# A three-group encoder layer on one core: the sums of a Strassen-like output product move from VectorE to GpSimd, ahead of the weight's low part

## What is computed

```python
h = rmsnorm(x, ln_gain[l])
proj = h @ w_in[l]
...
o_a = swa_sink_attention(q_a, k_a, v_a, q_norm_a[l], k_norm_a[l], sinks[l], bias)
o_c = short_gated_conv(b_c, c_c, x_c, conv_w[l])
mem_h = rmsnorm(mem, mem_ln_gain[l])
o_m = memory_cross_attention(q_m, mem_h, w_mem_kv[l], q_norm_m[l], k_norm_m[l])
mixed = jnp.concatenate([jax.nn.silu(g_a) * o_a,
                         jax.nn.silu(g_c) * o_c,
                         jax.nn.silu(g_m) * o_m], axis=-1)
x = x + mixed @ w_out[l]
```

## Time and profile before

| what | value |
|---|---|
| median of 3 runs | 2727.67 us (2726.12 to 2732.18) |
| the profiled execution | 2726.99 us |
| its span, first to last instruction | 2725.1 us |
| granted TensorE clock, mean | 0.996 of full speed |
| PE busy | 2666.0 us |
| DVE busy | 1686.9 us |
| POOL busy | 1496.5 us |
| ACT busy | 1101.5 us |

### The profile page before, as it was taken

How to read it: one execution, slowest core, us unless ns; L and a number is a source line. 1 busy time by engine, 2 the same in 40 slices (tenths; PEclk the granted TensorE clock), 3 DMA queues, 4 the chain that set the end, 5 groups by cost and what they waited for, 6 DMA issues and landing times.

```text
span 2725.1 us, 33717 instructions
## 1 busy us (share of the span) xinstructions
PE 2666.0 (98%) x12475; PEld 2198.8 (81%) x12475; DVE 1686.9 (62%) x2504; ACT 1101.5 (40%) x2435; POOL 1496.5 (55%) x1042
## 2 busy tenths in 40 slices
PE   6999999999999999999999999999999999999999
PEld 4888877888887778888877888888788788888887
DVE  4345775664476666456675754457642787867667
ACT  6333434442344344333434442343343444444443
POOL 5555644546554445555544455555454775756766
PEclk9999999999999999999999999999999999999999
DMA  7344443534344344334433434344245454444534
GB/s 216 122 138 124 159 135 97 174 110 161 106 138 151 112 143 142 129 119 140 159 120 113 155 124 139 113 132 151 92 150 168 157 199 146 167 150 140 174 118 140
DMA packets 234408, 383.16 MB, mean 141 GB/s; under 512 B 16822, under 2 KB 76292, under 8 KB 231940
## 3 DMA queue, kind: packets, MB, share of 16 engines
q1 hardware_dynamic: 189748, 274.05, 32.3%
q10 hardware_dynamic: 44496, 106.96, 11.1%
HBM read 308.86 MB, written 46.92 MB: 131 GB/s over the span
## 4 chain that ended last, share of the span: by engine, by line
PE 75%; DVE 13%; issue 3%; ACT 3%; DMA 2%; SPq 2%; POOL 1%; ACTq 0%; DVEq 0%
PE acc L1491 18%; PE acc L1493 17%; PE acc L1492 17%; DVE early L1146 4%; PE acc L1558 3%; PE acc L1562 3%; PE acc L1560 3%; ACT probs L779 1%; DMA probs_t<-blocks_t 1%; SPq L443 1%; PE ps_s L1615 1%; PE ps_o L1641 1%; DVE blocks_t L1221 1%; DMA raw<-in_w_mem_kv 1%; DVE a_lo L1362 1%
## 5 line engine op out<-in xcount | busy, mean ns | idle before, releaser
L536 POOL TENSOR_TENSOR w_lo<-raw,w_hi 128x512 fp32r<-128x512 f32 x928 | 1311.3, 1424 | 1168.6 <-ACT w_hi L620 1166.2
L620 ACT ACTIVATE w_hi<-raw 128x512 fp32r<-128x512 f32 x928 | 571.0, 628 | 1112.8 <-PE acc L1493 795.9
L1491 PE MATMUL acc<-h_hi,w_hi 128*128 128x512 f32 x1792 | 707.3, 395 | 12.8 <-POOL w_lo L536 10.7
L1492 PE MATMUL acc<-h_lo,w_hi 128*128 128x512 f32 x1792 | 700.4, 391 | 0.0
L1493 PE MATMUL acc<-h_hi,w_lo 128*128 128x512 f32 x1792 | 700.2, 391 | 0.0
L1491 PEld LDWEIGHTS acc<-h_hi,w_hi 128*128 128x128 f32 x1792 | 337.8, 188 | 91.6 <-POOL w_lo L536 13.8
L1493 PEld LDWEIGHTS acc<-h_hi,w_lo 128*128 128x128 f32 x1792 | 337.9, 189 | 70.9
L1492 PEld LDWEIGHTS acc<-h_lo,w_hi 128*128 128x128 f32 x1792 | 337.8, 189 | 68.7
L1491 PE MATMUL acc<-w_hi,h_hi 128*128 128x512 f32 (+1 forms) x1024 | 379.7, 371 | 0.0
L1493 PE MATMUL acc<-w_hi,h_lo 128*128 128x512 f32 (+1 forms) x1024 | 372.1, 363 | 0.0
L1492 PE MATMUL acc<-w_lo,h_hi 128*128 128x512 f32 (+1 forms) x1024 | 371.4, 363 | 0.0
(11 more groups left out here) (232 smaller groups left out, 3575.3 us busy)
## 6 DMA issues: line engine op xcount, KB each, us to landing
raw<-in_w_in SPq DMA_DIRECT2D x336, 512.0 KB, 4.0
raw<-w_sums SPq DMA_DIRECT2D x64, 512.0 KB, 3.9
probs_t<-blocks_t SPq DMA_DIRECT2D x384, 64.0 KB, 2.1
raw<-in_w_out SPq DMA_DIRECT2D x48, 512.0 KB, 3.6
stage<-in_w_out ACTq DMA_DIRECT2D x16, 1024.0 KB, 5.3
w_sums<-stage ACTq DMA_DIRECT2D x16, 1024.0 KB, 4.2
stage<-in_x ACTq DMA_DIRECT2D x16, 1024.0 KB, 5.1
mixed_rows<-ungated ACTq DMA_DIRECT2D x12, 1024.0 KB, 4.3
```

The costliest lines, as they stand in the source:

```text
L536: nc.gpsimd.tensor_tensor(w_lo[:, at, :], raw[:, slot_mod, HALF * half:HALF * half + HALF], w_hi[:, at, :].bitcast(F32), ALU.subtract).the ...
L620: nc.scalar.activation(w_hi[:, 2 * (slot_mod % 2) + half, :], raw[:, slot_mod, HALF * half:HALF * half + HALF], ACT.Copy).then_inc(hi_read ...
L1491: nc.tensor.matmul(dst, st[0], mv[0], start=first, stop=False)
L1492: nc.tensor.matmul(dst, st[0], mv[1], start=False, stop=False)
```

## The change

`a_sum` is taken from VectorE and given to GpSimd. It is called there ahead of `low` for the same slot. Its waits, its operands, and the semaphore that it raises stay as they were.

```diff
@@ gpsimd
+            def a_sum(j, h):
+
+                r, i, s = j // PAIR_SLOTS, j % PAIR_SLOTS // PRODUCT_SLOTS, j % PRODUCT_SLOTS
+                name, k = PRODUCTS[i][0], 2 * s + h
+                top, low = mixed_of[r // 2 * 2], mixed_of[r // 2 * 2 + 1]
+                s2 = low[:, k, :]
...
+                pool.wait_ge(s2_step, 16 * (r // 2 + 1))
+                pool.wait_ge(a_lo_ready, 2 * (j - 1) + h + 1)
+                nc.gpsimd.tensor_tensor(s_sum[:, h, :], *ins).then_inc(s_made, 1)
+
             for j in range(OUT_SLOTS):
                 if j + 2 < OUT_SLOTS:
+                    for h in range(2):
+                        a_sum(j + 2, h)
                     low((j + 2) % 4, OUT_BASE + j + 2)
@@ vector
-            def a_sum(j, h):
...
-                dve.wait_ge(s2_step, 16 * (r // 2 + 1))
-                dve.wait_ge(a_lo_ready, 2 * (j - 1) + h + 1)
-                nc.vector.tensor_tensor(s_sum[:, h, :], *ins).then_inc(s_made, 1)
...
                 if j + 2 < OUT_SLOTS:
-                    for h in range(2):
-                        a_sum(j + 2, h)
                     for h in range(2):
                         a_low(j + 2, h)
```

More of the change, by code:

```diff
@@ L587, in add_resid @@
                                         ALU.add).then_inc(resid_added, 1)
+            def a_sum(j, h):
[3 more added lines that the diff above has]
+                s2 = low[:, k, :]
+                if name == "S3":
+                    ins = (low[:, HALF_K + k, :], s2, ALU.subtract)
+                elif name == "S1":
+                    ins = (top[:, k, :], s2, ALU.add)
+                elif name == "S4":
+                    ins = (top[:, HALF_K + k, :], s2, ALU.subtract)
+                else:
+                    return
+                pool.wait_ge(s2_step, 16 * (r // 2 + 1))
+                pool.wait_ge(a_lo_ready, 2 * (j - 1) + h + 1)
+                nc.gpsimd.tensor_tensor(s_sum[:, h, :], *ins).then_inc(s_made, 1)
             for j in range(OUT_SLOTS):
                 if j + 2 < OUT_SLOTS:
+                    for h in range(2):
+                        a_sum(j + 2, h)
                     low((j + 2) % 4, OUT_BASE + j + 2)
```

## The result

The changed kernel takes 2758.43 us (median of 4 runs, 2754.93 to 2762.18) against 2729.26 us before (4 runs, 2726.12 to 2732.18). The ratio is 1.0107, with a 95% interval of 1.0086 to 1.0129. The forecast was 2756, range 2743 to 2776. The profiled execution took 2755.37 us with a span of 2753.6, against 2726.99 and 2725.1.

The account below looks back on a forecast made before the run. TensorE, busy 98% of the span, was taken as the bound. Late GpSimd costs 8.3 us a pair, 33.2 in four, less 4.9: +28.3 on 2726.99 gives 2755.3; with 0.7 for the median, 2756, range 2743 to 2776.

Parts of the forecast that it names:

- Price of an operation and of a collision: GpSimd in sum slots: 1.25 us an operation, plus 0.45 us for each VectorE operation with two SBUF inputs falling on it.
- The rival of full exclusion: GpSimd operations met by `a_lo`: each meeting costs the whole `a_lo`, 0.68 us; 30 us more, 2786; chance 0.03.
- First run: Slots 9 to 17 of a pair: 36 GpSimd operations and 17 meetings with `a_lo` make slot 19's low part 4.6 us late.
- Second run: Next eight slots, up to weight slot 27's low part: 32 GpSimd operations and 16 meetings with `a_lo`, 3.7 us late again.
- The credit: Output phase: relieving VectorE removes TensorE's losses around `a_lo`, 1.22 us in a pair, up to 4.9 us in four pairs.
- Absorbed: Output phase: GpSimd's idle time takes in the sums, no slot is late, 2722.8 us; chance 0.08.
- Late `stage` load: Slot 21: load lands after 6.7 us instead of 5.1, GpSimd waits, up to 1.6 us more a pair, 2762; chance 0.12.
- The case that the waits would name `a_lo`: Sum slots: TensorE waits for `a_lo`, not `w_lo`, with the same backlog and time; counted within the forecast's 0.75.
- At exactly twice VectorE's time: GpSimd sums priced at twice VectorE's 0.60 us instead of 1.25: 4.8 us less, 2751.

## Why the prediction was right

- **Price of an operation and of a collision.** Taken as 1.25 and 0.45 us. Measured: sums at 1.25, low parts at 3.40 for two, each met by one `a_lo`, so 0.45. The run without VectorE's `a_lo` shows the term by itself. The rival of full exclusion (0.68 us) is out. The Trainium skill's page "SBUF — State Buffer", section "Who interferes with whom", has the second instruction wait until the first has finished; that a collision costs time only with two SBUF inputs on VectorE agrees with the rows. That it would cost a whole `a_lo` does not: where every operation is met, one of each takes 1.70 us, less than 1.25 + 0.60.
- **First run.** Forecast: slot 13 is the first to wait, by 1.8 us, then 0.46 a slot, 4.6 us in all, and the product of slot 16 about 3 us later than before. Measured: a wait of 1.75 us at slot 13, slots of 5.90 us, 3.30 + 1.53 = 4.83 us, and 25.09 - 22.04 = 3.05 us.
- **Second run.** Forecast 3.7 us. Measured 0.34 + 3.35 = 3.69 us. The 0.34 stands in slots 20 to 23 and comes by a path that the prediction did not name: VectorE's PSUM additions of slot 20 wait for GpSimd's residual additions, and `a_lo` of slot 22 behind them. GpSimd has no idle time up to slot 25, so what TensorE loses there it should wait less at slot 25, and the sum stays as forecast; no run shows this by itself.
- **The credit.** Forecast 4.9 us. The kernel before lost 1.22 to 1.27 us a pair, and none of the waits for `a_lo` that it had in slot 26 is left. With the additions left out as well, the credit is what remains: 0.9981 x 2729 is 5 us below before (interval 1.9 to 8.5).
- **Sum.** Forecast +28.3, measured +29.2 by the medians and 29.9 by the slots. Most of what the slots have above the forecast is in the first run (4.83 for 4.6 us, four times) and in the first pair (0.7 us).
- **Rivals.** Absorbed: not so here, but right about where it would decide, since without collisions or additions it is so. Late `stage` load: it was issued at 2227.45 and landed in about 5.2 us (median after), that is about 2232.7, and GpSimd reached the addition at 2233.35:

```profile
2227.45 0.38 ACTq L970 DMA_DIRECT2D stage<-in_x  x1
```

```profile
2227.37 6.02 POOL L536 TENSOR_TENSOR w_lo<-raw,w_hi 128x512 fp32r<-128x512 f32 x4
2233.35 3.44 POOL L586 TENSOR_TENSOR xt<-xt,stage 128x512 f32<-128x512 f32 x2
```

  It fits by 0.6 us, about as forecast. The 6.7 us that this rival took from the earlier trace rows is the median of the stores of another tile; the load in question landed after 5.0 to 5.2 us in each of the four pairs. The case that the waits would name `a_lo` does not occur in this order, but it does with the low parts first.
- **"At exactly twice VectorE's time".** An estimate by the Trainium skill's "GPSIMD Engine Reference", section "Engine selection", would have been 2751 us. The rows keep 1.25 to 0.60, a little more than twice.

## What to carry to other kernels

Before moving work to an engine that looks half idle, count its operations from the last moment at which it waited to the first at which it is needed, and compare this with the time of the engine that it feeds. The average of the span says 59% while half of the 28 slots of a pair lose time. Price every meeting of a GpSimd operation with a VectorE operation of two SBUF inputs (here 0.45 us on top of the 1.25): 1.70 us for both is nearly the 1.25 + 0.60 that they take one behind the other, so moving one between these two engines does not take it off what they share, and here the cheaper engine should have it. And look at what stands in front of what in a queue: the same four operations in another order cost 19 us more through a ring over three engines.

## What was not expected, and what stays open

- That VectorE would be faster with more work (the kernel before with the additions on VectorE) was expected from the alternation. Its size is larger than forecast: by product starts the gain is 1.27 x 4 = 5 us, the medians give 8.7, the ratio's interval 5.7 to 12.6 us. The part above 5 us has no place in the output phase. Most of it goes with the granted clock of the executions, as far as five runs can tell. Each of the five runs, set against the mean of the runs of the kernel before with the same mean clock, is 4.2 to 7.2 us faster, 5.1 us in the mean (at 0.998, 2720.30 against 2724.94 and 2725.54). Four of the five had 0.995 or more, of the 24 runs of before only 11.
- In slots 24 to 27 of the first pair after the change, the 0.7 us more is the clock. TensorE waited 2.15 us before slot 25, and soon behind this wait its granted clock stood at 0.50, the level of 1.2 GHz, for 3.1 us. A matmul there starts every 0.43 us in place of 0.23 (columns of the second view: time, PE busy, granted clock, DMA share, GB/s):

```profile
2250.80 0.63 PE L1560 MATMUL ps_t<-w_lo,a_hi 128*128 128x512 f32 x1
2251.23 0.63 PE L1562 MATMUL ps_t<-w_hi,a_lo 128*128 128x512 f32 x1
```

```profile
2250.30:2253.40 3.10, 3.10 (x9) 0.50 0.31 97
```

  Slot 25 loses 1.73 us by it where the other pairs lose 0.46, and slots 26 and 27 then lose nothing. In the second pair the wait at slot 25 was as long (2.14 us) and the clock stayed at 1.00; why it fell in the one and not in the other stays open. With the low parts first, the clock stood at 0.50 in slot 25 of the fourth pair, too (for 5.5 us), and in the two traces with a longer beginning (additions left out, `a_lo` by ScalarE) at 0.50 and 0.54 in the first product. So the 8.52 us of the table is the price of the queue, and 0.7 us of the 29.9 came by the clock.
- Why the low parts first lose 0.45 us more in slots 16 to 19 of the first pair is not known.
